# Hybrid mixer and mixture-of-experts block on one core: last expert loads reordered, the last expert split in two products, experts 30 and 31 spread one at a time by row halves

## The chip, the cores and the metric

The kernel runs on one core of one Trainium2 chip. The metric is the device time of one execution in microseconds (us), as the median of several executions. Every input is float32.

## What is computed

One block over 256 tokens of width 1024 (plus 16 meta tokens in front): a token mixer (a pooling branch and a gated DeltaNet branch), then a mixture of 32 experts, then a last RMSNorm. The change touches only the experts and what follows them:

```python
for gi in range(N_EXPERT_GROUPS):                                   # 4 groups of 8 experts
    hdn = (jax.nn.silu(jnp.einsum('nd,edf->nef', xt, w_gate[gi]))   # d = 1024, f = 512
           * jnp.einsum('nd,edf->nef', xt, w_up[gi]))
    hdn = hdn * comb[:, gi, :, None].astype(hdn.dtype)              # top 2 experts of the top group
    y = y + jnp.einsum('nef,efd->nd', hdn, w_down[gi])
...
h = h + y
out = rmsnorm(h, norm_final_w)[:, N_META:]
```

## The kernel before, in words

Each engine has an instruction stream of its own, and they are tied together by counting semaphores written out by hand. The first part of the kernel, some 310 us, is the mixer and the router. What matters here is the second part, the loop over the 32 experts (numbers 0 to 31).

**The weights.** Each expert has three matrices of 2 MB: gate (c = 0), up (c = 1) and down (c = 2). The `ring` holds three experts. SyncE (SP) issues all loads on one queue, in the order of its own stream: for e from 3 on gate e, up e, and down e - 2. Each load first waits until the matrix three experts earlier has been used (`gu` counts finished gate and up products, `y` finished down products). Up 31 comes in 2 pieces, down 31 in 4, each piece with a semaphore of its own.

**One expert on TensorE.** Each expert has room for 64 tokens (`SLOTS`). The steps of the loop, in the order in which they stand in TensorE's stream for expert e, are:

- `gate_up(e)`: for each of 8 slices of the width, the gate product goes to rows 64 to 127 and the up product to rows 0 to 63 of bank 5. Stationary is a 128x64 tile of tokens, moving a 128x512 slice of weights, so the two products use different column halves of the array.
- `down(e - 2)`: the down product of two experts earlier (`LAG`), into the two row halves of bank 7.
- `turn_mid(e)`: 4 transposes of the hidden values `hmid`. They wait for ScalarE's Silu of the gate half and VectorE's product with the up half. ScalarE then copies the result to `hT`.
- `gather_next(e)`: part of the token gather for the next four experts. There is none for the last four.
- `turn_give` for odd e (2 transposes of the routing weights of a pair), or `spread(e/2 - 2)` for even e: it adds the weighted outputs of a pair of experts onto the residual stream in banks 0 to 3, 8 matmuls with the operand split in two parts (`yhi`, `ylo`).

ScalarE's `bring_y` copies a down product from bank 7 to `ysb` (rows 0 to 63 for the even expert of a pair, 64 to 127 for the odd one). For an even expert it first waits until the spread of the pair before has finished (semaphore `given`). `down(e)` waits until `bring_y` of the expert before it has emptied bank 7 (semaphore `ysb`).

**The end of the loop.** After `gate_up(31)`, `down(29)`, `turn_mid(31)` and `turn_give(15)` follow `down(30)`, `down(31)` (into bank 4), `spread(14)`, and `spread_last`: the pair 30 and 31 in one 128-row product in plain float32, 4 matmuls of 128x512, one for each bank. Each of these raises `closed`, and ScalarE's last norm (`square`, one call for each bank, then `root`) follows bank by bank; VectorE multiplies and scales beside it, and three stores end the kernel.

Of the kernel before, what the change touches and what calls it, by code (L numbers as in the profile page):

```python
# [36 lines left out]
ALU = mybir.AluOpType  # L37
# [49 lines left out]
YS = 2 * EXPERTS - 1  # L87
LAG = 2
SHORT = (EXPERTS - 1) % RINGS
# [323 lines left out]
def build_block(nc, x, meta_tokens, norm_mix_w, w_in, conv_w, pool_w, pool_scale, a_log, dt_bias, dn_norm_w,  # L413
# [3 lines left out]
    with ctx:  # L417
# [136 lines left out]
        ylast = ring[:, RING_AT[3 * ((EXPERTS - 2) % RINGS)], 0:D]  # L554
# [54 lines left out]
        hmid = lay_bench([FF])[0:SLOTS]  # L609
# [3 lines left out]
        hT = spare[:, D:D + (LAG + 1) * 4 * SLOTS].rearrange("p (n j s) -> p n j s", n=LAG + 1, j=4)  # L613
# [17 lines left out]
        share = xgT[:, 0, 0, :]  # L631
# [60 lines left out]
        def load_chunk(eng, e, c):  # L692
# [3 lines left out]
            if e == EXPERTS - 1 and c:  # L696
                parts, name = ((2, "last_up_land"), (4, "last_down_land"))[c - 1]
                dst2, src2 = (v.rearrange("p (s m) -> p s m", s=parts) for v in (dst, src))
                for n in range(parts):
                    eng.dma_start(dst2[:, n, :], src2[:, n, :]).then_inc(S(f"{name}{n}"), 16)  # L700
            else:
                eng.dma_start(dst, src).then_inc(S(f"w_land{3 * (e % RINGS) + c}"), 16)
# [19 lines left out]
        def _(sp):  # L722
# [59 lines left out]
            def one_pass(ps):  # L782
# [11 lines left out]
                if again:  # L794
                    sp.wait_ge(S("closed"), 4 * ps)
                    sp.sem_inc(S("reload"), 1)
# [28 lines left out]
        def _(act):  # L825
# [60 lines left out]
            for step in SEQ_OF["act"]:  # L886
# [21 lines left out]
                if kind == "aln":  # L908
                    act.wait_ge(S("a_chain"), 2)
                    nc.scalar.activation(plane(LN_), plane(E_), ACT.Ln, bias=1.0).then_inc(S("lnp"), 1)  # L910
# [86 lines left out]
                if kind == "ort":  # L997
                    h = step[1]
                    act.wait_ge(S("oss"), 3 * h + 3)
                    act.wait_ge(S("qe"), h + 1)  # L1000
# [56 lines left out]
            def one_pass(ps):  # L1057
# [3 lines left out]
                def bring_y(e):  # L1061
# [3 lines left out]
                    last = e == EXPERTS - 1  # L1065
                    act.wait_ge(S("y"), n + 1)
                    if g == 0 and e < EXPERTS - 2 and (again or pair):
                        act.wait_ge(S("given"), 2 * (pair + (PAIRS - 1) * ps))
                    if e == EXPERTS - 2 and again:
                        act.wait_ge(S("closed"), 4 * ps)  # L1070
                    to = ysb if e < EXPERTS - 2 else ylast
                    for half in range(1 if last else 2):
                        nc.scalar.activation(to[g * SLOTS:(g + 1) * SLOTS, half * 512:(half + 1) * 512],  # L1073
                                             pb[4 if last else 7][half * 64:half * 64 + SLOTS, :], ACT.Copy).then_inc(S("ysb"), 1)
                    if g == 1 and not last:

                        act.wait_ge(S("ysb"), YS * ps + 2 * e + 2)
                        act.wait_ge(S("give"), PAIRS * ps + (pair + 1))
                        for half in range(2):
                            nc.scalar.activation(yhi[:, half * 512:(half + 1) * 512], ysb[:, half * 512:(half + 1) * 512],  # L1080
                                                 ACT.Copy, scale=wslot[:, pair % 2:pair % 2 + 1]).then_inc(S("yhi"), 1)

                for e in range(EXPERTS):
# [4 lines left out]
                    if not first:  # L1088
                        act.wait_ge(S("hTp"), n)
                    nc.scalar.activation(hmid.rearrange("s (j p) -> s p j", j=4), pb[5][SLOTS:2 * SLOTS].rearrange("s (p j) -> s p j", j=4),  # L1090
                                         ACT.Silu).then_inc(S("sgate"), 1)

                    act.wait_ge(S("hTp"), n + 1)
                    if e >= LAG + 1:
                        act.wait_ge(S("y"), n - LAG)
                    elif again:
                        act.wait_ge(S("y"), base)
                    nc.scalar.activation(hT[:, e % (LAG + 1)], pb[6][:, 0:4 * SLOTS].rearrange("p (j s) -> p j s", j=4), ACT.Copy).then_inc(S("hT"), 1)  # L1098
# [5 lines left out]
                if not again:  # L1104
                    warm(ACT.Sqrt, 3)
                for e in range(EXPERTS - LAG, EXPERTS):
                    bring_y(e)
# [181 lines left out]
        def _(dve):  # L1289
# [38 lines left out]
            for step in SEQ_OF["dve"]:  # L1328
# [17 lines left out]
                if kind == "g":  # L1346
                    chain(V.tensor_scalar(plane(RL_), plane(X_), 0.0, None, ALU.max))
                    dve.wait_ge(S("lnp"), 1)
# [937 lines left out]
```

## Time and profile before

| | us |
|---|---|
| median of 3 runs (785.76 to 791.65) | 789.11 |
| the profiled execution's own time | 787.36 |
| its span (first to last instruction) | 785.6 |
| TensorE busy | 744.7 (95%) |
| VectorE, ScalarE, GpSimdE busy | 344.3, 334.2, 125.0 |
| moved by DMA | 240.94 MB |

The span is what the views of the trace cover; the execution's own time is 1.76 us more. In the views, PE is TensorE's matmul row and PEld its weight loads. A float32 matmul shows as two records, so 16 matmuls of the code are 32 records.

### The profile page before, as it was taken

The numbers are of one execution on the slowest core, as the hardware profiler recorded it, in microseconds if no ns is written. First come the engines' busy times: TensorE is split into PE (matmuls) and PEld (weight loads), VectorE is DVE, ScalarE is ACT, GpSimd is POOL, SyncE is SP. The second block draws the span as 40 slices with busy tenths as digits, with TensorE's granted clock in tenths as the row PEclk, the third lists the DMA queues.
The fourth block names the chain that finished last, engine by engine and source line by source line (L and its number), as shares of the span: only waits on it lengthen the run. The fifth ranks groups of instructions, "written<-read, shape, count | busy, mean of one in ns | idle before, by whom it ended". The sixth has DMA issues, their size and how long they took to land.

```text
span 785.6 us, 14136 instructions
## 1 busy us (share of the span) xinstructions
PE 744.7 (95%) x5557; PEld 475.5 (61%) x5557; DVE 344.3 (44%) x794; ACT 334.2 (43%) x632; POOL 125.0 (16%) x208
## 2 busy tenths in 40 slices
PE   8999999999999999999999999999899998998896
PEld 7989999989999987643443444344344343343332
DVE  4894787688585855722232223122122222112113
ACT  7876677676685744613122212222221221222224
POOL 7463242225432630000000000000000000000000
PEclk9999999999999999999999999999999999999999
DMA  8545564454754437999999999999999999999991
GB/s 208 139 130 144 146 153 129 125 149 112 185 139 130 124 116 281 428 423 425 430 426 429 426 427 428 427 429 428 426 428 427 425 428 430 428 426 429 425 398 63
DMA packets 80233, 240.94 MB, mean 307 GB/s; under 512 B 6817, under 2 KB 65298, under 8 KB 67874
## 3 DMA queue, kind: packets, MB, share of 16 engines
q1 hardware_dynamic: 79858, 239.19, 79.8%
q8 instruction: 47, 0.77, 0.4%
q10 hardware_dynamic: 304, 0.79, 0.3%
q14 instruction: 24, 0.20, 0.1%
HBM read 238.92 MB, written 1.05 MB: 305 GB/s over the span
## 4 chain that ended last, share of the span: by engine, by line
PE 70%; DMA 23%; DVE 4%; issue 1%; ACT 1%; SPq 0%; DVEq 0%; ACTq 0%
DMA ring<-in_expert_w_up_dram 23%; PE banks L1803 21%; PE banks L2143 20%; PE banks L2205 7%; PE banks L1998 2%; PE banks L2080 2%; PE banks L2154 2%; PE banks L1922 1%; PE banks L1935 1%; PE banks L1983 1%; PE banks L2180 1%; PE banks L1939 1%; PE banks L1926 1%; PE banks L1960 1%; PE banks L1944 1%
## 5 line engine op out<-in xcount | busy, mean ns | idle before, releaser
L2143 PE MATMUL banks<-ring,bench 128*64 128x512 f32 x1024 | 234.9, 613 | 22.2 <-DMA ring<-in_expert_w_up_dram 20.5
L1803 PE MATMUL banks<-rounded 128*128 128x256 f32 (+3 forms) x1344 | 199.1, 295 | 2.4 <-DVE desk L1457 1.4
L1803 PEld LDWEIGHTS banks<-rounded 128*128 128x128 f32 (+1 forms) x1344 | 171.4, 188 | 6.4 <-issue 1.6
L2143 PEld LDWEIGHTS banks<-ring,bench 128*64 128x64 f32 x1024 | 77.8, 140 | 160.0 <-issue 155.6
L1700 DVE TENSOR_TENSOR bench<-banks,bench 64x512 f32<-64x512 f32 x32 | 33.6, 1051 | 260.8 <-ACT bench L1090 260.8
L1090 ACT ACTIVATE bench<-banks 64x512 f32<-64x512 f32 x32 | 34.1, 1066 | 211.3 <-PE banks L2143 211.3
L2205 PE MATMUL banks<-ring,spare 128*64 128x512 f32 x512 | 115.5, 592 | 0.8 <-issue 0.8
L2205 PEld LDWEIGHTS banks<-ring,spare 128*64 128x64 f32 x512 | 39.5, 137 | 70.7 <-issue 70.7
L853 ACT ACTIVATE rounded<-room 128x1024 fp32r<-128x1024 f32 x64 | 67.5, 1054 | 21.8 <-PE banks L1803 15.0
L1321 DVE TENSOR_TENSOR rounded<-room,rounded 128x1024 fp32r<-128x1024 f32 x49 | 66.3, 1353 | 14.7 <-ACT rounded L853 13.7
L1190 POOL TENSOR_TENSOR rounded<-room,rounded 128x256 fp32r<-128x256 f32 x60 | 43.8, 760 | 60.8 <-ACT rounded L853 60.6
L1073 ACT ACTIVATE ysb<-banks 64x512 f32<-64x512 f32 x60 | 35.5, 591 | 36.4 <-PE banks L2154 35.3
L1098 ACT ACTIVATE spare<-banks 128x256 f32<-128x256 f32 x32 | 12.3, 384 | 85.8 <-PE banks L2180 85.8
L1663 DVE TENSOR_TENSOR bench<-banks,gain 128x512 f32<-128x512 f32 x30 | 20.7, 691 | 62.1 <-PE banks L2080 61.6
L1372 DVE SCALAR_TENSOR_TENSOR desk<-banks,prmT,desk 128x271 f32<-128x271 f32 (+5 forms) x72 | 35.3, 491 | 5.2 <-ACT desk L863 3.1
L2080 PE MATMUL banks<-hot,xhi 128*128 128x256 f32 x112 | 31.2, 312 | 0.0
L2080 PE MATMUL banks<-hot,xlo 128*128 128x256 f32 x112 | 27.7, 282 | 0.0
L2180 PEld LDWEIGHTS banks<-ident,bench 64*128 64x128 f32 x128 | 10.3, 138 | 25.0 <-issue 24.3
L2154 PE MATMUL banks<-yhi,give 128*128 128x512 f32 x60 | 23.8, 397 | 0.0
L2154 PE MATMUL banks<-ylo,give 128*128 128x512 f32 x60 | 23.5, 392 | 0.0
L2080 PEld LDWEIGHTS banks<-hot,xhi 128*128 128x128 f32 x112 | 21.1, 188 | 2.2 <-issue 0.5
L1215 POOL TENSOR_TENSOR room<-room 96x96 f32<-96x96 f32 x32 | 16.7, 531 | 33.5 <-PE banks L1922 22.7
(289 smaller groups left out, 876.6 us busy)
## 6 DMA issues: line engine op xcount, KB each, us to landing
ring<-in_expert_w_gate_dram SPq DMA_DIRECT2D x31, 2048.0 KB, 27.6
ring<-in_expert_w_up_dram SPq DMA_DIRECT2D x30, 2048.0 KB, 31.7
ring<-in_expert_w_down_dram SPq DMA_DIRECT2D x30, 2048.0 KB, 35.2
room<-in_w_in_dram SPq DMA_DIRECT2D x56, 512.0 KB, 4.2
ring<-in_expert_w_down_dram SPq DMA_DIRECT2D x8, 512.0 KB, 9.9
room<-in_w_out_dram SPq DMA_DIRECT2D x8, 512.0 KB, 3.3
ring<-in_expert_w_gate_dram SPq DMA_DIRECT2D x4, 512.0 KB, 7.8
ring<-in_expert_w_up_dram SPq DMA_DIRECT2D x4, 512.0 KB, 7.2
```

The lines of the kernel that those rows point to most:

```text
L853: nc.scalar.activation(whi[:, n % HI_SLOTS], win[:, n % WIN_SLOTS].rearrange("p k c -> p (k c)"), ACT.Copy).then_inc(S("whi"), 1)
L1073: nc.scalar.activation(to[g * SLOTS:(g + 1) * SLOTS, half * 512:(half + 1) * 512], pb[4 if last else 7][half * 64:half * 64 + SLOTS, :], A ...
L1090: nc.scalar.activation(hmid.rearrange("s (j p) -> s p j", j=4), pb[5][SLOTS:2 * SLOTS].rearrange("s (p j) -> s p j", j=4), ACT.Silu).then_ ...
L1190: ins = nc.gpsimd.tensor_tensor(wlo[:, lo_slot(n), cols], w[:, cols], whi[:, n % HI_SLOTS, cols].bitcast(F32), ALU.subtract)
L1321: V.tensor_tensor(wlo[:, lo_slot(n)], w, whi[:, n % HI_SLOTS].bitcast(F32), ALU.subtract).then_inc(S("wlo"), 1)
L1372: ins = V.scalar_tensor_tensor(acc[:, i, f + sh:L], p[:, 0:L - f - sh], prmT[:, tap * 24 + col:tap * 24 + col + 1], acc[:, i, f + sh:L], A ...
L1700: V.tensor_tensor(hmid.rearrange("s (j p) -> s p j", j=4), pb[5][0:SLOTS].rearrange("s (p j) -> s p j", j=4), hmid.rearrange("s (j p) -> s ...
L1803: ins = T.matmul(o, a, b[:, k, lo_at:L], start=(k == 0 and n == 0), stop=(k == KT - 1 and n == 2))
L2080: ins = T.matmul(pb[4][:, k * WIDE:(k + 1) * WIDE], x[:, t, ch:ch + P], hot[:, t, :], start=(t == 0 and x is xhi), stop=(t == TT - 1 and x ...
L2143: ins = T.matmul(pb[5][(1 - c) * SLOTS:(2 - c) * SLOTS, :], xgT[:, q % ROOMS, kt, j * SLOTS:(j + 1) * SLOTS], w[c][:, kt, :], start=(kt == ...
L2154: ins = T.matmul(pb[2 * t + half], gives[i % 2][:, t * P:(t + 1) * P], y[:, half * 512:(half + 1) * 512], start=False, stop=True, skip_gro ...
L2205: ins = T.matmul(pb[4 if e == EXPERTS - 1 else 7][half * 64:half * 64 + SLOTS, :], hT[:, e % (LAG + 1), j, :], w[:, j, half * 512:(half + ...
```

## The change

- SP issues down 29 ahead of gate 31 and up 31. Up 31 comes in 4 pieces, down 30 in 2, down 31 in 4.
- For expert 30, `turn_mid(30)` stands ahead of `down(28)`. A third `turn_give` is added, since experts 30 and 31 get their routing weights one at a time (`weights(e, e)` fills both halves with the same expert).
- `gate_up(31)` becomes `product_last(0)` (gate, bank 5) and `product_last(1)` (up, bank 4), each with 128x256 moving slices, so that the 512 hidden columns lie as two halves over 128 partitions. Silu and the product then run on 128x256 instead of 64x512, and `turn_mid(31)` is 2 full transposes.
- `down(29)` moves ahead of the last expert's products, and `spread(14)` ahead of `turn_mid(31)`.
- `spread_last` is replaced by `spread_alone(0)` for expert 30, between `down(30)` and `down(31)`, and `spread_alone(1)` for expert 31. In each the output columns 0 to 511 lie in rows 0 to 63 and columns 512 to 1023 in rows 64 to 127, and the 4 matmuls have 64 rows each.
- `hT` has 4 places instead of 3. A few semaphores of the first part share a counter. Nothing else of the first part is changed.

```diff
-YS = 2 * EXPERTS - 1
+YS = 2 * EXPERTS - 2
+GIVES = PAIRS + 1
+HTS = LAG + 2
+PIECES = {(EXPERTS - 1, 1): 4, (EXPERTS - 1, 2): 4, (EXPERTS - 2, 2): 2}
...
-                for e in range(RINGS, EXPERTS + LAG):
-                    if e < EXPERTS:
-                        load(e, 0)
-                        load(e, 1)
+                for e in range(RINGS, EXPERTS - 1):
+                    load(e, 0)
+                    load(e, 1)
                     if e - LAG >= RINGS:
                         load(e - LAG, 2)
+                load(EXPERTS - 3, 2)
+                load(EXPERTS - 1, 0)
+                load(EXPERTS - 1, 1)
+                load(EXPERTS - 2, 2)
+                load(EXPERTS - 1, 2)
...
+                def bring_last(g):
+
+                    act.wait_ge(S("y"), base + EXPERTS - 1 + g)
...
+                    nc.scalar.activation(ylasts[g], pb[7 - 2 * g][:], ACT.Copy).then_inc(S("ysb"), 1)
...
-                    if e >= LAG:
+                    if LAG <= e < EXPERTS - 1:
                         bring_y(e - LAG)
+                    if e == EXPERTS - 2:
+                        bring_y(EXPERTS - 3)
...
-                def spread_last():
+                def product_last(c):
+
+                    e = EXPERTS - 1
+                    if c == 0:
...
+                        landed(e, 0)
+                    w = ring[:, RING_AT[3 * (e % RINGS) + c], :].rearrange("p (k q h j) -> p k h q j", k=KT, h=2, j=2)
+                    for kt in range(KT):
+                        if c == 1 and kt % (KT // PIECES[e, 1]) == 0:
+                            piece(e, 1, kt // (KT // PIECES[e, 1]))
+                        for half in range(2):
+                            ins = T.matmul(pb[5 - c][half * 64:half * 64 + SLOTS, 0:FF // 2], xgT[:, e // 4 % ROOMS, kt, e % 4 * SLOTS:(e % 4 + 1) * SLOTS],
+                                           w[:, kt, half], start=(kt == 0), stop=(kt == KT - 1), skip_group_check=True)
+
+                def spread_alone(g):
+
+                    pe.wait_ge(S("give"), GIVES * ps + PAIRS + g)
+                    pe.wait_ge(S("ysb"), YS * (ps + 1) - 1 + g)
+                    for t in range(TT):
+                        for half in range(2):
+                            rows = slice(half * SLOTS, (half + 1) * SLOTS)
+                            ins = T.matmul(pb[2 * t + half], shares[g][rows, t * P:(t + 1) * P], ylasts[g][rows],
+                                           start=False, stop=True, skip_group_check=True)
...
+                    elif e == EXPERTS - 2:
+                        turn_mid(e)
+                        down(e - LAG)
...
+                down(EXPERTS - 3)
+                product_last(0)
+                product_last(1)
+                spread(PAIRS - 2)
+                turn_mid(EXPERTS - 1)
+                turn_give(GIVES, EXPERTS - 1)
                 down(EXPERTS - 2)
+                spread_alone(0)
                 down(EXPERTS - 1)
-                spread(PAIRS - 2)
-                spread_last()
+                spread_alone(1)
```

TensorE, from `gate_up(30)` on. The lines of the kernel before are L2143 `gate_up`, L2205 `down`, L2180 `turn_mid` and L2151 the start of `spread(13)`:

```order
L2143 MATMUL banks<-ring,bench 64x512 x16
L2197 REGISTER_ALU
L2205 MATMUL banks<-ring,spare 64x512 x8
L2172 REGISTER_ALU
L2180 MATMUL banks<-ident,bench 128x64 x4
L2151 REGISTER_ALU
```

The same place after the change. L2172 is `gate_up`, L2228 `turn_mid`, L2257 `down`, L2239 `turn_give`, and L2178 and L2180 the start of `spread(13)`:

```order
L2172 MATMUL banks<-ring,bench 64x512 x16
L2217 REGISTER_ALU
L2228 MATMUL banks<-ident,bench 128x64 x4
L2248 REGISTER_ALU
L2257 MATMUL banks<-ring,spare 64x512 x8
L2236 REGISTER_ALU
L2239 MATMUL banks<-ident,bench 128x128 x2
L2178 REGISTER_ALU
L2180 REGISTER_ALU
```

`turn_mid(30)` now follows its own gate and up products directly, `down(28)` comes behind it, and two transposes are added. After the spread before, `gate_up(31)` came next; now it is `down(29)`.

TensorE at the end, in the kernel before, from `turn_mid(31)` (L2180) over `turn_give` (L2188) and both down products to the start of `spread(14)`:

```order
L2180 MATMUL banks<-ident,bench 128x64 x4
L2188 MATMUL banks<-ident,bench 128x128 x2
L2197 REGISTER_ALU
L2205 MATMUL banks<-ring,spare 64x512 x16
L2151 REGISTER_ALU
```

The same after the change, from `turn_mid(31)` (L2231) on. L2210 is `spread_alone`:

```order
L2231 MATMUL banks<-ident,bench 128x2x64 x2
L2236 REGISTER_ALU
L2239 MATMUL banks<-ident,bench 128x128 x2
L2248 REGISTER_ALU
L2257 MATMUL banks<-ring,spare 64x512 x8
L2206 ISA
L2210 MATMUL banks<-ring,bench 128x512 x4
L2257 MATMUL banks<-ring,spare 64x512 x8
L2210 MATMUL banks<-ring,bench 128x512 x4
```

The two down products are pulled apart by one small spread, and `spread(14)`, which stood between `down(31)` and the last spread, is gone from here.

## Rows read from the trace of the kernel before

**Rows 1.** The page: DMA rate in GB/s, 40 equal slices of the span.

```profile
GB/s 208 139 130 144 146 153 129 125 149 112 185 139 130 124 116 281 428 423 425 430 426 429 426 427 428 427 429 428 426 428 427 425 428 430 428 426 429 425 398 63
```

**Rows 2.** The chain that ended last, in order of time: start us, us, what.

```profile
702.87 35.55 DMA ring<-in_expert_w_up_dram
...
738.56 8.78 PE banks L2143 x32
747.34 3.43 PE banks L2205 x16
750.77 0.39 PE banks L2180 x4
751.16 2.04 PE banks L2154 x8
753.20 7.02 PE banks L2143 x32
760.22 3.43 PE banks L2205 x16
763.65 0.40 PE banks L2180 x4
...
764.08 0.39 ACT spare L1098
...
764.61 0.41 PE banks L2188 x2
765.02 0.78 issue
765.79 7.09 PE banks L2205 x32
772.88 2.04 PE banks L2154 x8
774.92 3.45 PE banks L2166 x8
```

**Rows 3.** Copy, Silu and product beside that chain: start us, us, engine line op.

```profile
747.38 1.06 ACT L1090 ACTIVATE bench<-banks 64x512 f32<-64x512 f32 x1 [9.57 <-PE banks L2143]
...
748.47 1.05 DVE L1700 TENSOR_TENSOR bench<-banks,bench 64x512 f32<-64x512 f32 x1 [9.76 <-ACT bench L1090]
...
753.30 1.21 ACT L1073 ACTIVATE ysb<-banks 64x512 f32<-64x512 f32 x2 [1.71 <-PE banks L2154]
...
764.49 1.21 ACT L1073 ACTIVATE ysb<-banks 64x512 f32<-64x512 f32 x2
```

**Rows 4.** The same view, where nothing stood between a product and its transposes (expert 1).

```profile
337.01 7.09 PE L2143 MATMUL banks<-ring,bench 128*64 128x512 f32 x32
...
346.36 0.46 PE L2180 MATMUL banks<-ident,bench 64*128 64x64 f32 x4 [0.26 <-DVE bench L1700]
```

**Rows 5.** The same view, ScalarE in the last norm.

```profile
775.82 0.60 ACT L1119 ACTIVATE bench<-banks 128x512 f32<-128x512 f32 x1 [2.31 <-PE banks L2166]
...
778.19 0.30 ACT L1124 ACTIVATE rs<-rs,eps 128x1 f32<-128x1 f32 x1
...
778.39 0.60 ACT L1119 ACTIVATE bench<-banks 128x512 f32<-128x512 f32 x1
```

**Rows 6.** SP's issues of down 29 and 30 (first row) and down 31.

```profile
719.77 15.01 SPq L702 DMA_DIRECT2D ring<-in_expert_w_down_dram  x2
750.82 1.76 SPq L700 DMA_DIRECT2D ring<-in_expert_w_down_dram  x4
```

**Rows 7.** Stretches: busy us of PE, PEld, DVE, ACT, POOL; then PEclk, DMA share, GB/s.

```profile
739.00:740.00 1.00, 1.00 (x4) 0.30 (x2) 0.00 (x0) 0.00 (x0) 0.00 (x0) 0.50 0.96 410
...
743.00:744.00 1.00, 1.00 (x8) 0.37 (x5) 0.00 (x0) 0.00 (x0) 0.00 (x0) 1.00 1.04 442
...
767.00:768.00 1.00, 1.00 (x8) 0.38 (x6) 0.89 (x2) 0.98 (x2) 0.00 (x0) 1.00 0.07 29
```

**Rows 8.** TensorE's timeline: products after waits for their weights, in brackets the wait.

```profile
590.69 8.78 PE L2143 MATMUL banks<-ring,bench 128*64 128x512 f32 x32 [2.05 <-DMA ring<-in_expert_w_up_dram]
...
679.86 8.78 PE L2143 MATMUL banks<-ring,bench 128*64 128x512 f32 x32 [1.91 <-DMA ring<-in_expert_w_up_dram]
...
723.89 7.09 PE L2143 MATMUL banks<-ring,bench 128*64 128x512 f32 x32 [1.73 <-DMA ring<-in_expert_w_up_dram]
```

More of the change, by code:

```diff
@@ L608, in build_block @@
         junk2 = bench[:, KT * WIDE + TT * 18 * 32:KT * WIDE + TT * 18 * 32 + D]
[L609 removed]
+        hmid_all = lay_bench([FF])
+        hmid = hmid_all[0:SLOTS]
         hotw = lay_bench([TT, 2, SLOTS])
@@ L1064, in bring_y @@
                     pair, g = e // 2, e % 2
-                    last = e == EXPERTS - 1
                     act.wait_ge(S("y"), n + 1)
-                    if g == 0 and e < EXPERTS - 2 and (again or pair):
+                    if g == 0 and (again or pair):
                         act.wait_ge(S("given"), 2 * (pair + (PAIRS - 1) * ps))
[L1069 to L1075, printed above, removed]
+                    for half in range(2):
+                        nc.scalar.activation(ysb[g * SLOTS:(g + 1) * SLOTS, half * 512:(half + 1) * 512],
+                                             pb[7][half * 64:half * 64 + SLOTS, :], ACT.Copy).then_inc(S("ysb"), 1)
+                    if g == 1:
                         act.wait_ge(S("ysb"), YS * ps + 2 * e + 2)
-                        act.wait_ge(S("give"), PAIRS * ps + (pair + 1))
+                        act.wait_ge(S("give"), GIVES * ps + (pair + 1))
                         for half in range(2):
@@ L1673, in lower, with weights @@
                                                ALU.mult, ALU.subtract).then_inc(S("ylo"), 1)
+                def weights(a, b, turned_before):
+                    if again or a:
+                        dve.wait_ge(S("givep"), turned_before)
+                    for t in range(TT):
+                        for f, e in enumerate((a, b)):
+                            ins = V.tensor_scalar(hotw[:, t, f, :], iota_c[:], plan[:, e, t:t + 1], plan[:, e, TT + t:TT + t + 1], ALU.is_equal, ALU.mult)
+                    ins.then_inc(S("hotw"), 1)
                 if again:
@@ L1697, in one_pass @@
                         slots_of(q + 1)
-                    dve.wait_ge(S("sgate"), experts + (e + 1))
-                    V.tensor_tensor(hmid.rearrange("s (j p) -> s p j", j=4), pb[5][0:SLOTS].rearrange("s (p j) -> s p j", j=4),
-                                    hmid.rearrange("s (j p) -> s p j", j=4), ALU.mult).then_inc(S("hmid"), 1)
-                    if g == 0:
-                        if again or i:
-                            dve.wait_ge(S("givep"), pairs + i)
-                        for t in range(TT):
-                            for f in range(2):
-                                ins = V.tensor_scalar(hotw[:, t, f, :], iota_c[:], plan[:, e + f, t:t + 1], plan[:, e + f, TT + t:TT + t + 1], ALU.is_equal, ALU.mult)
-                        ins.then_inc(S("hotw"), 1)
+                    alone = e >= EXPERTS - 2
@@ L2120, in landed, with piece @@
                         return
+                    short = sum(k == c and n % RINGS == e % RINGS for n, k in PIECES)
                     loads = ps * (uses(EXPERTS, e % RINGS, RINGS) - short) - (e % RINGS == 0)
                     pe.wait_ge(S(f"w_land{3 * (e % RINGS) + c}"), 16 * (loads + (e // RINGS + 1)))
+                def piece(e, c, n):
+                    pe.wait_ge(S(f"piece_land{e}_{c}_{n}"), 16 * ps + 16)
                 def gate_up(e):
@@ L2236, in one_pass @@
                         turn_mid(e)
-                    if g:
-                        turn_give(i)
-                    elif i >= 2:
+                    if g or e == EXPERTS - 2:
+                        turn_give(i + 1, e)
+                    if g == 0 and i >= 2:
                         spread(i - 2)
```

143 lines of the change are left out of this document (80 added, 63 removed).

## The prediction

> **What bounds the kernel now.** I first read the DMA rate over the span [rows 1]. From about 310 us on it stays at 425 to 430 GB/s, and it falls only in the last slice: the expert loads run without a hole. Then I read the chain that ended last [rows 2]. Up to 738.56 us it runs through the landing of an up matrix; the last one is up 30. After that no transfer is in it. `gate_up(30)` starts at 738.56, and up to the end of `spread_last` (774.92 + 3.45 = 778.37) the chain is TensorE's own stream, but for a copy on ScalarE (0.39) and one wait of 0.78. The last norm and the stores take 785.6 - 778.37 = 7.23 more.
>
> Do the other loads matter? A matrix of 2.10 MB at 428 GB/s takes 4.9 us. Counted on from up 30 (landed at about 738.4) in the order of issue, down 28 lands at 743.3, gate 31 at 748.2, up 31 at 753.1, down 29 at 758.0, down 30 at 762.9 and down 31 at 767.8. The transfers do fade out in the stretch 767 to 768 [rows 7], so the estimate holds. TensorE takes gate and up 31 at 753.20 (half of up 31 is enough then), down 29 at 760.22, down 30 at 765.79 and down 31 some 3.5 us later [rows 2]. The smallest slack is 2.2 us, at down 29. So the end of the kernel is bound by **TensorE's order and its waits on ScalarE and VectorE**, from 738.56 on. The part before is bound by the stream of loads, and the change leaves that alone up to up 30.
>
> **The loads: 0.** Down 29 was issued at 719.77 [rows 6], when `down(26)` was done. Now gate 31 and up 31 queue behind that wait instead of ahead of it, and are issued about 3 us later. The queue has work until down 28 lands at 743.3, so nothing starves. The new landings are down 29 at 748.2, gate 31 at 753.1, up 31 at 758.0, and the others as before. Down 31 waits for `down(28)`, which ends some 3 us later than the 750.8 of before [rows 2, 6]; the queue holds down 30 until 762.9. The cover is 9 us or more. If it were gone, down 31 would come up to 3 us later, and the timeline below still leaves it 9 us. The extra issues on SP hide in the same backlog.
>
> **TensorE after 747.34, step by step.** I write the new order down with the durations of [rows 2].
>
> 1. Wait for `hmid` of expert 30. Before, `down(28)` (3.43) covered Silu and the product (1.06 + 1.05, [rows 3]). Now `turn_mid(30)` is next. Expert 1 shows the naked wait: products end at 344.10, transposes start at 346.36 [rows 4]. **+2.26.**
> 2. `turn_mid(30)` 0.40, `down(28)` 3.43, `spread(13)` 2.04: as before. The additional `turn_give` costs **+0.41**. This brings us to 755.9.
> 3. `down(29)` is next, and it needs bank 7 emptied by `bring_y(28)`, which waits for `given`, that is for the end of `spread(13)`. Before, this copy (753.30, 1.21, [rows 3]) lay under `gate_up(31)`, 7.02 us. Now nothing lies between: 0.10 to the start, 1.21, and 0.09 back to TensorE (764.49 + 1.21 to 765.79). **+1.40**, `down(29)` ends at 760.7.
> 4. The two products have 16 matmuls each of half the columns. If 256 columns take half of 512, they take 7.02 together: 0, ending at 767.7. Silu (now 128 lanes, about 0.55) lies under the second product, and the multiply and `lower(14)` lie under `spread(14)`, which ends at 769.8. Uncovered, Silu and multiply would cost 1.1.
> 5. `turn_mid(31)` 0.40, the copy to `hT` 0.55 with its gaps, `turn_give` 0.41, all as before. The wait of 0.78 ahead of `down(30)` was for `bring_y(29)` (its copy ends at 765.70, [rows 3]); now that copy lies under `product_last(0)`: **-0.78**.
> 6. `down(30)` 3.5, then `spread_alone(0)` needs a copy of bank 7 at once: 0.04 + 0.60 + 0.14 (0.60 is one 128x512 of the last norm, [rows 5], the 0.14 is the gap from the copy ending at 764.47 to 764.61, [rows 2]). **+0.78.** Its four matmuls come on top.
> 7. `down(31)` 3.5, and again a naked copy before `spread_alone(1)`; before, `spread(14)` hid it. **+0.78.**
>
> **The row-half spreads** have no row in this trace. Bounds: the four 128-row matmuls took 3.45 [rows 2], which is the price if two 64-row matmuls don't run together. If they do, it is half, 1.72. The nearest row for that is `gate_up`: its two column halves run together, since 32 records take 7.02, or 0.22 each, where 8 records of `spread_last` take 0.43 each at the same 512 columns. I take 1.72. The Trainium skill, "TensorEngine Tiling (Array Packing)", section "Key Properties", says that tiles work independently, for matmuls as for weight loads; no run here shows it for row tiles yet. The same section says that changing the tiling mode drains the engine, which speaks against this change, since it changes mode more often at the end. The chain has no gap at such a change (`down(31)` to `spread(14)` at 772.88, [rows 2]), so the row says 0; by the rule the sum would be some tenths of a us higher. Then `spread_alone(0)` is **+1.72**, and `spread_alone(1)` instead of `spread_last` **-1.73**.
>
> **The last norm.** Before, the banks were closed 0.86 apart, and ScalarE kept pace: first square 775.82, root 778.19, last square 778.39 [rows 5], just behind the last matmul at 778.37. From first square to last there are 2.57 us of work that ScalarE and VectorE can't shorten. If the banks close in pairs, the first is ready only 0.86 before the end T, so the last square starts at T - 0.84 + 2.57 = T + 1.73, not at T + 0.02: **+1.71**. With serial row halves this term is 0.
>
> Sum: 2.26 + 0.41 + 1.40 - 0.78 + 0.78 + 0.78 + 1.72 - 1.73 + 1.71 = **+6.55**. Against the profiled execution, 787.36, that is 793.9. This execution lies 1.75 below the median 789.11, so the forecast for the median is 789.11 + 6.5 = **795.6**, 0.8% slower. One per cent, 7.9 us, is about what a measurement of this kernel can tell from no change.
>
> **Rivals.**
>
> - **The clock falls in the new wait.** After waits of 1.91 us and more the products ran 8.78 instead of 7.09, with the granted clock at 0.50, the lower level of 1.2 GHz [rows 7, 8]; after 1.73 us they did not. The same happened at 738.56. The new wait of 2.26 falls among those that cost 1.69. Against it: the clock was given back by 743 [rows 7] and TensorE was busy until 747.3, and the wait is followed by four transposes only. Sum 8.2, so 797.4. I give 28%.
> - **The row halves run one after the other**, so the change doesn't do what it is written for. Then 6.55 + 1.72 + 1.73 - 1.71 = 8.3, or 797.4, and 10.0 with the clock: 799.1. For it: no row shows row halves together. Against: column halves do. 18%.
> - **Strided weights.** The last products read pairs of columns out of every four. If a 256-column slice took as long as 512 contiguous ones, +7.0: 802.6. The trace shows no such read on TensorE. The bounds are 0 and 7.0, and I take 0, for half the columns. 3%.
> - **Not slower: the last loads come late.** If the transfers behind up 30 lagged by L us, the kernel before would wait from L = 2.2 on (down 29 behind gate and up 31), while the new order waits only from 7.6 on (gate 31 lands at 753.1 and is needed at 760.7). At L = 7.6 the kernel before has lost 5.4 and the new one nothing, so the change costs 6.5 - 5.4 = 1.1: 790.2, no difference. It decides from about L = 6 on. Against it: a steady 428 GB/s to the end [rows 1], and transfers that fade at 767 to 768 as counted. Even this doesn't make the new kernel faster. 5%.
>
> **How the numbers follow.** The forecast case has 42%, the clock 28, serial halves 18, strided weights 3, late loads 5. The last 4 are for waits smaller than I count (+2 to +4). The range 792.5 to 800.0 takes in the first three cases but for half of the doubly bad one, with about 3 us below the forecast for the scatter of a median whose runs spread over 5.9 us. Slower by over 1% means above 797.0: a tenth of the forecast case, 60% of the clock case, most of the serial case and the strided one make 0.41. Faster by over 1% has no mechanism that I can name, 0.04. The rest, 0.55, is within 1%.
>
> **What the profile after would show.** Step 1: `turn_mid(30)` starts about 2.3 us after the end of `gate_up(30)`, with VectorE named as what released it. Step 3: `down(29)` starts about 1.4 after `spread(13)`, and the copy between them is released by the spread. Step 4: each last product 3.5 us. Steps 6 and 7: gaps of 0.8 ahead of both small spreads, and 1.7 (together) or 3.4 (serial) for each. The last square starts 1.7 after the last matmul, or at once if serial. The clock between 749 and 756 tells the first rival. `gate_up(30)` itself should start near 738.5; if it moved, the front or the stream changed, which I count at 0. The forecast is wrong if a transfer ends any wait after `gate_up(30)`, or if TensorE's stream from there to the last matmul is not about 4.8 us longer.

## The result, and the profile after

| | before | after |
|---|---|---|
| median of 6 runs each | 790.38 us (785.68 to 793.76) | 798.36 us (793.13 to 802.93) |
| the profiled execution, its span | 787.36, 785.6 | 798.72, 797.0 |

The ratio is **1.0099**, with a 95% interval of 1.0061 to 1.0138: the change made the kernel slower by 1.0%, some 8 us. The forecast was 6.5 us slower (0.8%). One of the ten timed runs of experiment 1 further down took 945.42 us at a mean granted clock of 0.735, where the others show 0.976 to 0.985, and is left out of its ratio.

The chain of the kernel after, from `gate_up(30)` on, in order of time (start us, us, what), answers to [rows 2]. L2172 is `gate_up`, L1103 Silu, L1733 the product with up, L2228 and L2231 `turn_mid`, L2257 `down`, L2239 `turn_give`, L2183 `spread`, L2199 `product_last`, L1093 the copy `bring_last`, L2210 `spread_alone`:

```profile
739.79 9.96 PE banks L2172 x32
...
749.76 1.04 ACT bench L1103
...
750.83 1.03 DVE bench L1733
...
751.91 0.46 PE banks L2228 x4
752.37 5.28 PE banks L2257 x16
757.65 0.37 PE banks L2239 x2
758.02 1.85 PE banks L2183 x8
759.86 1.40 issue
761.27 3.65 PE banks L2257 x16
764.92 7.25 PE banks L2199 x64
772.17 2.04 PE banks L2183 x8
774.22 0.23 PE banks L2231 x2
...
775.00 0.41 PE banks L2239 x2
775.41 3.61 PE banks L2257 x16
...
779.04 0.61 ACT ring L1093
...
779.79 1.99 PE banks L2210 x8
781.77 3.61 PE banks L2257 x16
...
785.40 0.60 ACT ring L1093
```

There are five places where TensorE isn't in the chain or waits: behind `gate_up(30)`, 1.40 ahead of `down(29)` ("issue": the view names nothing that it waited for), the copy of `hT` (as before), and a copy ahead of each small spread. No transfer stands behind `gate_up(30)`.

ScalarE's and TensorE's timeline of the last norm, to be read against [rows 5]:

```profile
786.14 1.99 PE L2210 MATMUL banks<-ring,bench 64*128 64x512 f32 x8 [0.79 <-ACT ring L1093]
787.27 0.60 ACT L1137 ACTIVATE bench<-banks 128x512 f32<-128x512 f32 x1 [1.27 <-PE banks L2210]
...
789.57 0.29 ACT L1142 ACTIVATE rs<-rs,eps 128x1 f32<-128x1 f32 x1
...
789.77 0.58 ACT L1137 ACTIVATE bench<-banks 128x512 f32<-128x512 f32 x1
```

The last matmul ends at 786.14 + 1.99 = 788.13, and the last square (789.77) starts 1.64 later, where it started 0.02 later before.

Stretches of 1 us (busy us of PE, PEld, DVE, ACT, POOL, then granted clock, DMA share, GB/s), to be read against [rows 7]:

```profile
744.00:745.00 1.00, 1.00 (x6) 0.34 (x4) 0.00 (x0) 0.00 (x0) 0.00 (x0) 0.50 0.96 410
...
753.00:754.00 1.00, 1.00 (x5) 0.24 (x3) 0.00 (x0) 0.00 (x0) 0.00 (x0) 0.50 0.99 397
```

The clock was at its lower level (0.50, 1.2 GHz) until past 745, longer than before, and once more in `down(28)`, 753 to 755.

I cut the span of every kernel at three points: the start of `gate_up(30)`, its end, and the end of the last matmul (start plus length of the last group of records). For the kernel before that is 738.56, 747.34 and 778.37 [rows 2].

| kernel | `gate_up(30)` starts | it takes | from there to the last matmul | from there to the end |
|---|---|---|---|---|
| before | 738.56 | 8.78 | 31.03 | 7.23 |
| after | 739.79 | 9.96 | 38.39 | 8.87 |
| difference | +1.23 | +1.18 | +7.36 | +1.64 |

The first difference is chance: up 30 landed between 737.1 and 743.5 in all 13 profiles of this study, early and late for either order of the last experts. Most of that scatter is older than the expert loop. The first product of the loop, `gate_up(0)`, starts between 325.7 and 332.1, and from there to the landing it takes 410.9 to 412.1 us in every profile. The three late landings (743.0 to 743.5, experiments 5, 6 and 7; all others come by 739.8) have their delay from the mixer, where the granted clock fell: 0.50 in the stretch from 60 to 65 us, against 0.98 to 1.00 in the other ten. At 50.2 us the chains of the kernel before and of experiment 7 are still level; a group of TensorE that starts at 68.78 in the first starts at 73.20 in the second. The pages show it in the fourth slice, first in the kernel before, then in that of experiment 7:

```profile
PEclk9999999999999999999999999999999999999999
PEclk9997999999999999999999999999999899999998
```

The second difference is chance too: without filling `gate_up(30)` took 8.40 to 9.96 in eight profiles, 8.78 and 9.90 with TensorE's order of before and 8.40 to 9.96 with the changed one. The other two belong to the change, but for what the clock does in `down(28)`. That scatter is why the last two columns carry the verdicts below, and the timed medians only where an effect is large. Experiments 2 to 5 have one execution each, so their total times show nothing by themselves.

### The profile page after: what moved, and what is told of

The parts are those of the page before. It is cut to its first block, busy times and chain, and to the rows that moved or that the text cites. A ratio compares the mean times of both kernels' runs of the same rounds, so it can differ in the third digit from the quotient of the medians.

```text
span 797.0 us, 14223 instructions
## 1 busy us (share of the span) xinstructions
PE 749.1 (94%) x5597; PEld 480.0 (60%) x5597; DVE 344.4 (43%) x798; ACT 333.0 (42%) x631; POOL 124.9 (16%) x208
## 4 chain that ended last, share of the span: by engine, by line
PE 68%; DMA 23%; DVE 4%; issue 2%; POOL 1%; ACT 1%; SPq 0%; DVEq 0%; POOLq 0%; ACTq 0%
DMA ring<-in_expert_w_up_dram 22%; PE banks L1831 20%; PE banks L2172 20%; PE banks L2257 8%; PE banks L2026 2%; PE banks L2183 2%; PE banks L2108 2%; PE banks L1950 1%; PE banks L1963 1%; PE banks L2011 1%; PE banks L2199 1%; PE banks L2228 1%; PE banks L1967 1%; PE banks L1954 1%; PE banks L1988 1%
## 5 line engine op out<-in xcount | busy, mean ns | idle before, releaser
L2172 PE MATMUL banks<-ring,bench 128*64 128x512 f32 x992 | 228.9, 615 | 23.1 <-DMA ring<-in_expert_w_up_dram 21.4
L2172 PEld LDWEIGHTS banks<-ring,bench 128*64 128x64 f32 x992 | 76.4, 141 | 156.9 <-issue 154.1
L1733 DVE TENSOR_TENSOR bench<-banks,bench 64x512 f32<-64x512 f32 x31 | 32.5, 1050 | 251.9 <-ACT bench L1103 251.9
L1103 ACT ACTIVATE bench<-banks 64x512 f32<-64x512 f32 x31 | 33.0, 1065 | 207.7 <-PE banks L2172 207.7
L2257 PE MATMUL banks<-ring,spare 128*64 128x512 f32 x512 | 117.5, 600 | 1.4 <-issue 1.4
L2257 PEld LDWEIGHTS banks<-ring,spare 128*64 128x64 f32 x512 | 39.7, 138 | 72.0 <-issue 72.0
L2108 PE MATMUL banks<-hot,xhi 128*128 128x256 f32 x112 | 31.2, 312 | 0.0
L2228 PEld LDWEIGHTS banks<-ident,bench 64*128 64x128 f32 x124 | 10.0, 138 | 26.5 <-issue 22.7
L1690 DVE SCALAR_TENSOR_TENSOR ylo<-ysb,bench,yhi 128x512 fp32r<-128x512 f32 x30 | 21.2, 748 | 8.3 <-ACT yhi L1085 8.3
L2183 PE MATMUL banks<-yhi,give 128*128 128x512 f32 x60 | 23.8, 397 | 0.0
L2183 PE MATMUL banks<-ylo,give 128*128 128x512 f32 x60 | 23.5, 392 | 0.0
```

The lines of the kernel that those rows point to most:

```text
L1733: V.tensor_tensor(hmid.rearrange("s (j p) -> s p j", j=4), pb[5][0:SLOTS].rearrange("s (p j) -> s p j", j=4), hmid.rearrange("s (j p) -> s ...
L2108: ins = T.matmul(pb[4][:, k * WIDE:(k + 1) * WIDE], x[:, t, ch:ch + P], hot[:, t, :], start=(t == 0 and x is xhi), stop=(t == TT - 1 and x ...
L2172: ins = T.matmul(pb[5][(1 - c) * SLOTS:(2 - c) * SLOTS, :], xgT[:, q % ROOMS, kt, j * SLOTS:(j + 1) * SLOTS], w[c][:, kt, :], start=(kt == ...
L2183: ins = T.matmul(pb[2 * t + half], gives[i % 2][:, t * P:(t + 1) * P], y[:, half * 512:(half + 1) * 512], start=False, stop=True, skip_gro ...
L2257: ins = T.matmul(pb[5 if e == EXPERTS - 1 else 7][half * 64:half * 64 + SLOTS, :], hT[:, e % HTS, j, :], w[:, j, half * 512:(half + 1) * 512],
```

## The experiments

**1. The load order alone**, in the kernel before.

```diff
+                for e in range(RINGS, EXPERTS - 1):
+                    load(e, 0)
+                    load(e, 1)
...
+                load(EXPERTS - 3, 2)
+                load(EXPERTS - 1, 0)
+                load(EXPERTS - 1, 1)
+                load(EXPERTS - 2, 2)
+                load(EXPERTS - 1, 2)
```

> The kernel before with only the load order of the change (down 29 issued ahead of gate 31 and up 31), everything on TensorE as before. Theory (loads have slack in the changed kernel only because down(29) stands ahead of the last products there): here TensorE asks for gate 31 and half of up 31 about 14.7 us after up 30 landed, and that half now lands 3.5 matrices of 4.9 us behind up 30, at about 17.2 us. So a wait of about 2.4 us for up 31 appears at the last gate and up products, and from the end of gate_up(30) to the last matmul it takes about 33.4 us instead of 31.0 (less if the clock falls at gate_up(30) for longer). Rival (the load order is free wherever it stands, as the prediction counted it): 31.0. Second rival (the new order brings something): under 31.0.

Measured: 791.33 against 788.69, ratio 1.0028 (0.9999 to 1.0057). TensorE's timeline shows the two `gate_up` of experts 30 and 31:

```profile
739.38 9.90 PE L2148 MATMUL banks<-ring,bench 128*64 128x512 f32 x32 [3.84 <-DMA ring<-in_expert_w_up_dram]
...
756.56 7.09 PE L2148 MATMUL banks<-ring,bench 128*64 128x512 f32 x32 [1.41 <-DMA ring<-in_expert_w_up_dram]
```

The wait for up 31 is there. It is 1.41 and not 2.4 because `gate_up(30)` took 9.9, 1.1 us longer, so that TensorE asked later. To the last matmul it took 781.79 - 749.28 = 32.5, which is 31.0 + 1.4. So the load order has a price where gate and up 31 stand ahead of `down(29)`, and none in the changed kernel, where they stand behind it. It brings nothing by itself. The changed kernel with the old load order was not run.

**2. `down(28)` ahead of `turn_mid(30)` again**, in the changed kernel.

```diff
-                        turn_mid(e)
                         down(e - LAG)
+                        turn_mid(e)
```

> The changed kernel with down(28) put back ahead of turn_mid(30). Theory: the wait of 2.2 us behind gate_up(30) goes, and with it the fall of the clock in down(28), which took 5.28 us instead of 3.43. From the end of gate_up(30) to the last matmul 38.4 - 2.2 - 1.85 = 34.3 us. Rival (the wait is only the first of several limits, and a wait for bank 7 or for a landing takes its place): 36 to 38, with a new wait of over 1 us in the chain before spread(14).

Measured in one execution: 791.22. From 745.64 to 780.56 it took **34.9**. The chain:

```profile
745.64 3.43 PE banks L2257 x16
749.07 0.41 PE banks L2228 x4
...
750.44 1.85 PE banks L2183 x8
752.29 1.40 issue
```

No wait behind `gate_up(30)`, and no fall of the clock: `down(28)` took 3.43. (The changed order itself ran without a fall in two of four profiles, see experiment 6, so the second point could be chance.) The 0.6 above the expectation has a place: `turn_give` now stands directly behind `turn_mid(30)` and waits for the `hT` copy (0.39 and 0.14 in the chain), which `down(28)` covered before. Clear of the clock this move is worth 36.7 (experiment 6) - 34.9 = 1.8.

**3. `product_last(0)` ahead of `down(29)`.**

```diff
-                down(EXPERTS - 3)
                 product_last(0)
+                down(EXPERTS - 3)
                 product_last(1)
```

> The changed kernel with product_last(0) moved ahead of down(29), so that it covers the copy of bank 7 that down(29) waits for. Theory: the wait of 1.40 us ahead of down(29) goes and nothing replaces it: 38.4 - 1.4 = 37.0 us from the end of gate_up(30) to the last matmul, or 35.1 if the clock doesn't fall in down(28) this time. Rival: Silu of the last expert now queues on ScalarE behind the copies of down(29), so that the multiply is late and a wait of about 1 us appears ahead of turn_mid(31): no gain.

Measured in one execution: 791.87, and 781.18 - 745.96 = **35.2**, with `down(28)` at 3.58, so the clock didn't fall this time. The chain:

```profile
752.54 1.85 PE banks L2183 x8
754.38 3.77 PE banks L2199 x32
758.16 3.43 PE banks L2257 x16
761.59 3.63 PE banks L2199 x32
```

The 1.40 is gone and nothing took its place. Clear of the clock the move is worth 36.7 - 35.2 = 1.5. The rival with the late Silu falls: `turn_mid(31)` follows the spread without a wait.

**4. Both down products ahead of the small spreads.**

```diff
                 down(EXPERTS - 2)
-                spread_alone(0)
                 down(EXPERTS - 1)
+                spread_alone(0)
                 spread_alone(1)
```

> The changed kernel with down(31) moved ahead of spread_alone(0), so that down(31) covers the copy of expert 30's output and spread_alone(0) that of expert 31's. Theory: both gaps of 0.78 go: 38.4 - 1.6 = 36.8 us from the end of gate_up(30) to the last matmul, 35.0 if the clock doesn't fall in down(28). The last norm stays at 8.9 us behind the last matmul. Rival (the price lies in the row-half matmuls and the changes of tiling mode, not in the waits for the copies): a gain of under 0.5 us.

Measured in one execution: 796.22, and 785.52 - 749.25 = **36.3**, of which 1.6 is again a fall of the clock in `down(28)` (5.22). TensorE's timeline at the end:

```profile
781.82 3.70 PE L2210 MATMUL banks<-ring,bench 64*128 64x512 f32 x16
```

Both spreads run without a gap. The gain is 2.1 (38.4 - 36.3, both with the fall): 1.55 for the two gaps, and 0.5 because 16 records in a row take 3.70 and not twice 1.99, and the two down products 7.02 and not 7.22. So the rival is right in a small part: breaking up rows of like matmuls costs too, in sum 0.5 us.

**5. The small spreads by token tile**, on top of 4.

```diff
                 down(EXPERTS - 2)
                 down(EXPERTS - 1)
-                spread_alone(0)
-                spread_alone(1)
+                for t in range(TT):
+                    for g in range(2):
+                        spread_alone(g, [t])
```

> The changed kernel with both down products first and then the small spreads by token tile: both experts onto banks 0 and 1, then both onto banks 2 and 3. Theory (the last norm is 1.6 us longer because the banks close in pairs and only 1 us before the end, while ScalarE and VectorE need 2.6 us from the first square to the last): the first pair now closes 2 us before the end, so from the last matmul to the end of the span it takes 8.9 - 1.0 = 7.9 us. From the end of gate_up(30) to the last matmul as in the kernel with both down products first, 36.8 or 35.0. Rival (the last norm is longer for another reason, such as the copy or the closing semaphores of 64-row matmuls): 8.9 stays.

Measured in one execution: 796.08. The last matmul ends at 782.60 + 3.70 = 786.30 and the span at 794.4: **8.1** instead of 8.9. That the first pair closes late is shown as the cause of half of the 1.6 that the last norm was longer. The other half is the pairing itself, as ScalarE's rows argue. The first square of token tile 1, in the kernel before and here:

```profile
777.53 0.60 ACT L1119 ACTIVATE bench<-banks 128x512 f32<-128x512 f32 x1 [0.17 <-PE banks L2166]
...
786.34 0.60 ACT L1137 ACTIVATE bench<-banks 128x512 f32<-128x512 f32 x1 [0.25 <-PE banks L2210]
```

Before, bank 2 was closed one matmul ahead of bank 3, and this square started 0.84 ahead of the end of the last matmul (778.37). Here both close together, it starts 0.04 behind the end, and VectorE's product (L1768, 0.69) and the second square follow it. No run tests this half by itself. To the last matmul it took 34.6, without a fall of the clock.

**6. TensorE kept busy in the two waits**, in the changed kernel. The small matmuls do no work of the reference. The lines stand at the head of `gate_up`, and with 8 instead of 10 at the head of `turn_mid`.

```diff
+                    if e == EXPERTS - 2:
+                        for _ in range(10):
+                            T.matmul(pb[4][:, 0:P], ones[:], ones[:], start=True, stop=True)
```

> The changed kernel with 10 small matmuls that do no work (128x128 of ones into the idle bank 4) ahead of gate_up(30) and 8 more ahead of turn_mid(30), so that TensorE isn't idle in these two waits. Theory (the fall of the granted clock is caused by the idle wait ahead of it): granted clock at the higher level in both places, gate_up(30) 7.0 us instead of 9.96, down(28) 3.4 instead of 5.28; from the end of gate_up(30) to the last matmul 36.5 instead of 38.4. Rival (the clock falls for another reason, for example the load of the DMA stream or what ran before): both durations stay long.

Measured: 794.23 against 788.23, ratio 1.0067 (1.0028 to 1.0106). TensorE's timeline:

```profile
740.15 2.40 PE L2162 MATMUL banks<-ones 128*128 128x128 f32 x20
743.11 7.09 PE L2175 MATMUL banks<-ring,bench 128*64 128x512 f32 x32 [0.56 <-DMA ring<-in_expert_w_up_dram]
750.13 2.05 PE L2222 MATMUL banks<-ones 128*128 128x128 f32 x16
752.42 0.46 PE L2234 MATMUL banks<-ident,bench 64*128 64x64 f32 x4 [0.24 <-DVE bench L1733]
752.81 3.65 PE L2263 MATMUL banks<-ring,spare 128*64 128x512 f32 x16
```

7.09 and 3.65: both products ran at the higher clock. From 750.21 to 786.95 it took **36.7**, which is what the changed order takes with the clock left out. In the four changed kernels with the wait of 2.18 and nothing in it (after and 3 to 5), `down(28)` took 5.28, 3.58, 5.22 and 3.58: the clock fell in two of four.

So the two places differ in what is shown. Ahead of `gate_up(30)`, all eight profiles without filling took 8.40 to 9.96 and all five with it (this one and experiments 7 and 9 to 11) 7.09: there the filling keeps the clock. Ahead of `turn_mid(30)`, one filled profile without a fall stands against two of four without filling, and the first filling had changed `gate_up(30)` as well. That the filling helps there is not shown.

**7. The same filling in the kernel before**, ahead of `gate_up(30)` only.

> The kernel before with 10 small matmuls that do no work ahead of gate_up(30). Theory: gate_up(30) takes 7.0 us instead of 8.78, with nothing given back, since the landings behind up 30 have 2 us of slack: the span is 1.7 us shorter for the same landing of up 30, 0.2%, at the edge of what rounds can show. Rival (TensorE then runs into the landings): a wait for down 29 or up 31 of about 1 us appears and the gain is halved.

Measured: 786.34 against 788.23, ratio 0.9982 (0.9956 to 1.0008), which agrees with -0.2% and doesn't show it. The timeline does:

```profile
739.34 2.40 PE L2130 MATMUL banks<-ones 128*128 128x128 f32 x20
743.59 7.09 PE L2146 MATMUL banks<-ring,bench 128*64 128x512 f32 x32 [1.86 <-DMA ring<-in_expert_w_up_dram]
```

7.09 instead of 8.78, and 31.0 from there to the last matmul: nothing is given back to the landings.

**8. All moves of 2 to 5 together**, in the changed kernel.

> The changed kernel with all four moves: down(28) ahead of turn_mid(30), product_last(0) ahead of down(29), both down products ahead of the small spreads, these by token tile. Theory (the costs are separate waits and add up): from the end of gate_up(30) to the last matmul 38.4 - 1.85 - 2.2 - 1.4 - 1.6 = 31.4 us, from there to the end 7.9: in sum about 1 us more than the kernel before (31.0 + 7.2). A landing may end a wait of up to 1.3 us at product_last(0) if gate_up(30) runs at full clock, since TensorE then asks for gate 31 before it has landed. Rival (they overlap): 33 or more.

Measured: 790.73 against 788.23, ratio 1.0027 (0.9997 to 1.0058), so this kernel and the one before can't be told apart by their times. From 748.43 to 776.09 + 3.71 = 779.80 it took **31.4**, and 8.1 from there to the end. The sum, 39.5, is 1.2 us above the kernel before. The waits are separate and add up: the single gains of 1.8, 1.5 and 2.1 (experiments 2 to 4) taken from 36.7 give 31.3. That the expected 31.4 was met to a tenth is luck in part, since it left out the `hT` copy that experiment 2 had uncovered (0.55) and the 0.5 that like products in a row give back (experiment 4). What remains lies in the last norm (+0.9) and in TensorE's own stream (+0.3).

**9. A version that could beat both**, from the kernel before: filled as in 7, and the two 128-row spreads at the end by token tile: for each t, `spread_two` adds first `spread(14)` and then the last pair onto banks 2t and 2t + 1.

```diff
-                spread(PAIRS - 2)
-                spread_last()
+                spread_two()
```

> The kernel before with 10 small matmuls that do no work ahead of gate_up(30), and at the end spread(14) and the last spread (both with 128 rows) taken by token tile: banks 0 and 1 are closed before banks 2 and 3 are begun. Theory: gate_up(30) takes 7.1 us instead of 8.78; from its end to the last matmul 31.0, since the copies now have 1.0 us of cover and need 0.8; from the last matmul to the end 6.3 instead of 7.2, since the first token tile's norm is done by then. From the landing of up 30 to the end of the span 44.6 us, where the kernel before took 47.2: 0.3% of the time. Rival (the norm is bound by the last squares alone): 7.2 stays. Rival (the copies of the last output come too late for the first token tile): 31.8 instead of 31.0.

Measured: 787.93 against 788.68, ratio 0.9995 (0.9965 to 1.0024). `gate_up(30)` took 7.09, then 31.2 (777.11 - 745.93), then 784.4 - 777.11 = **7.3**: the number is the first rival's, and the norm gained nothing. The reason is another than the rival's, as experiment 11 shows. The timeline here:

```profile
776.29 0.60 ACT L1119 ACTIVATE bench<-banks 128x512 f32<-128x512 f32 x1 [1.10 <-PE banks L2190]
...
776.88 0.28 ACT L1124 ACTIVATE rs<-rs,eps 128x1 f32<-128x1 f32 x1
...
778.01 0.75 DVE L1760 TENSOR_SCALAR late<-late,rs 128x1024 f32<-128x1024 f32 x1
```

The root of token tile 0 (776.88) waits behind the first square of tile 1 on ScalarE, though its sum was made at 775.83. So VectorE scales tile 0 only at 778.01, between the last sum and the last product.

**10. Down 31 loaded and multiplied ahead of down 30**, on top of 9.

```diff
-                down(EXPERTS - 2)
                 down(EXPERTS - 1)
+                down(EXPERTS - 2)
                 spread_two()
```

The loads of the two swap places too, down 30 comes in 4 pieces, and ScalarE copies in the new order.

> The kernel of the run above, with down 31 loaded and multiplied ahead of down 30 (down 30 now in 4 pieces), so that the wait of 0.78 us for the emptying of bank 7 ahead of down(30) is covered by down(31), which writes bank 4. Theory: 0.78 less, and about 0.3 of it back, because both copies of expert 30's output (1.2 us on ScalarE) are now the last ones and have 1.0 us of cover: from the end of gate_up(30) to the last matmul 30.5 us. Rival (a landing takes the wait's place, since down 30 is now the last load and lands 29.4 us behind up 30): 31.0 to 32, with the wait named as a DMA.

Measured: 786.04 against 788.68, ratio 0.9975 (0.9948 to 1.0001). From 745.07 to 775.87 it took **30.8**: the 0.78 ahead of the down products is gone, and the last copy gives 0.28 of it back:

```profile
771.26 1.95 PE L2193 MATMUL banks<-ring,bench 128*128 128x512 f32 x4 [0.28 <-ACT ring L1076]
```

No landing took its place.

**11. The norm's order mended**, on top of 10.

```diff
-                square(1, 0)
                 root(0)
+                square(1, 0)
                 square(1, 1)
```

On VectorE the inverse and the scaling of tile 0 go ahead of the products of tile 1 in the same way.

> The kernel of the run with down 31 first, with the last norm's order changed to fit: on ScalarE the root of token tile 0 ahead of the first square of token tile 1, on VectorE the scaling of token tile 0 ahead of the products of token tile 1. Theory (the end stayed at 7.3 us behind the last matmul because the root of tile 0 stood behind a square of tile 1, so that the scaling of tile 0, 0.67 us in the chain, came between the last sum and the last product): that piece leaves the chain, and from the last matmul to the end it takes 6.7 us instead of 7.3. From the end of gate_up(30) to the last matmul 30.8 as before. In the timed runs 0.6 us or 0.1% can't be told. Rival (the chain is the squares, sum, root and stores alone): 7.3 stays.

Measured: **785.58 against 789.53, ratio 0.9958 (0.9932 to 0.9985)**, the only version that is faster than the kernel before beyond its interval. Experiments 10 and 11 were not timed side by side; what the last step alone is worth is read from the trace. The timeline:

```profile
774.05 1.88 PE L2193 MATMUL banks<-ring,bench 128*128 128x512 f32 x4
...
774.84 0.29 ACT L1127 ACTIVATE rs<-rs,eps 128x1 f32<-128x1 f32 x1 [0.82 <-DVE rs L1748]
775.11 0.60 ACT L1122 ACTIVATE bench<-banks 128x512 f32<-128x512 f32 x1
...
775.37 0.75 DVE L1761 TENSOR_SCALAR late<-late,rs 128x1024 f32<-128x1024 f32 x1
```

The scaling of tile 0 starts at 775.37, before the last matmul ends at 775.93, and the span ends 6.5 us later instead of 7.3. Together: 7.09 + 30.7 + 6.5 = 44.3 us from the start of `gate_up(30)`, against 47.0 before.

## Why the prediction was right

The measured 798.36 lies in the range, and the direction and the mechanism held. The sum, +6.5, was 1.3 us below the 7.8 of the ratio, within its interval (4.8 to 10.9 us). The forecast of 795.6 was 2.8 too low: 1.3 of that is the kernel before, which took 790.38 in these runs and not 789.11, and 1.5 the change. The range was wide enough for both. By the prediction's own sign, a stream about 4.8 us longer, it was off: 7.36 in the profile, of which 1.7 is the clock rival, and 5.7 without it. By its own terms:

- **What bounds the kernel**: right. No transfer ended a wait behind `gate_up(30)` before or after. One reading was off: the rate falls to 398 GB/s in the slice before the last already [rows 1]. The transfers faded at 767 to 768 as counted, so nothing hangs on it.
- **The loads, 0**: right in the changed kernel. But the cover is `down(29)` standing first. Without that, experiment 1 shows a wait of 1.41 for up 31. The prediction didn't ask what the load order would cost by itself.
- **Steps 1 and 3**, the waits for `hmid` (+2.26) and for `given` and the copy (+1.40): 751.91 - 749.74 = 2.17 and 1.40 in the profile. Undoing each by itself returned 1.8 and 1.5 of the 36.7 (experiments 2 and 3), the first less because it uncovers the `hT` copy.
- **Step 2**, the added `turn_give`: 0.37, but the spread behind it then took 1.85 instead of 2.04, so 0.2 in sum and not 0.41.
- **The down products** behind transposes or a wait: `down(28)` 3.58 (without the fall) and `down(29)` 3.65, not the 3.43 that they take directly behind `gate_up`, 0.37 in both. The prediction took the 3.43 over.
- **Step 4**, the halved products: 7.25 instead of 7.02. The rival with strided weights falls.
- **Step 5**, -0.78: right; `down(30)` starts with `turn_give`'s end at 775.41. `turn_mid(31)` took 0.23 and not 0.40.
- **Steps 6 and 7**: the gaps are 0.77 each. The term that was mis-sized is **the row-half spreads: 1.99 each, not 1.72**, 0.54 in both. The records show that the row halves run together (8 in 1.99, 0.25 each, against 0.43 for `spread_last`). The Trainium skill, "TensorEngine Tiling (Array Packing)", section "Key Properties", says that tiles work independently, and these rows agree. The 1.72 holds inside a group: in experiment 4, 16 records in a row took 3.70, so eight more added 1.71. What was missing is some 0.28 once for each group. The down products likewise take 7.22 in two groups against 7.09 in one.
- **The last norm**, +1.71: 1.64. Experiment 5 moved it by 0.8 by closing the first pair earlier. The prediction took the order of the norm's steps as given. In a kernel that closes token tile 0 earlier, experiment 11 took 0.8 off the norm by that order alone; in the changed kernel it was not tried.
- **The clock rival** (28%) came true in the profiled execution: 5.28 - 3.58 = 1.7 of the 7.36 us, where it had counted 1.69. It isn't certain in each execution: two of four. Both times `gate_up(30)` had run long too (9.96 and 9.78, against 8.44 and 8.46). A long `gate_up(30)` alone doesn't do it: in experiment 1 it took 9.90, and `down(28)`, with no wait between, took 3.62 in TensorE's timeline, where the kernel before has 3.63. So in these few profiles the fall came only with the wait, and the wait alone was not enough. The line that the prediction drew between 1.73 and 1.91 [rows 8] isn't one either: in the traces of the later runs waits for a landing from 1.92 to 2.89 were followed by 7.09 as well as by 8.4 and more.

The deviations in TensorE's stream add up: +0.37 for the down products, -0.24 for step 2 by experiment 6 (0.37 + 1.84 instead of 0.41 + 2.04), +0.23 for step 4, -0.17 for `turn_mid(31)`, +0.13 for the down products in two groups and +0.54 for the row-half spreads make +0.86, and the stream without the fall was 36.74 - 31.03 = 5.7 us longer where the sum has 4.84. So the forecast was near also because some terms were too high where others were too low. With the norm the cost is 36.7 + 8.9 - 31.0 - 7.2 = 7.4 us without the clock. If the fall comes in half of the executions, as in two of four, that adds 0.8 on average: 8.2, an estimate, against the 7.8 of the ratio. The serial row halves and the late loads didn't happen.

What stays open is why the clock falls in some executions and not in others, both in `down(28)` and in the mixer, from where the late landings of up 30 come. The timed runs fit: those of the kernel before over 793 us have a mean granted clock of 0.973 to 0.979, those under 787 us one of 0.985 to 0.992. No experiment was made on the mixer.

## What to carry to other kernels

At the end of a kernel, list for each product what empties its bank, what prepares its operand, and what TensorE does meanwhile. A move that looks neutral by TensorE's own work can uncover such handovers, here four of 0.8 to 2.2 us, and here they added up one for one. Closing outputs in pairs costs time if the engine that finishes them takes them one by one, here 1.6 us; it must get the first early, and its own order must let the first tile be finished before the second comes. Judge a load order together with the order of use: the same order cost 1.41 us of waiting in one kernel and none in the other. And where the total scatters by 6 us, cut the traces at the same event and compare the pieces.

## What was not expected of the hardware

- 2.4 us of small matmuls at the start of a wait of over 4 us for a landing were enough to keep the clock at its higher level, even with 1.86 us of idling behind them (experiment 7), although after a wait of 1.91 alone it was low in the kernel before [rows 8]. It was so in all five filled profiles (7.09) and in none of the eight others (8.40 to 9.96).
- In four of 13 profiles the granted clock fell in the mixer, between 56 and 58 us of the span. In three of them it came back only at 67 to 71 us, and everything behind came some 4 to 6 us later. In the stretch from 50 to 55 us TensorE had been idle for 1.0 to 1.4 us in all 13.
- Matmuls on row halves ran together at 0.25 us a record in a group of 8 (1.99), and 0.23 in a group of 16 (3.70), against 0.43 for full rows.
